# Cross-attention's output projection: a signal for each half unit, both additions ahead of both low parts, and the MLP norm's sum one unit later

## The reference

```python
u = rms_norm_2(h, norm_xattn_g[l])
mem_n = rms_norm_2(mem, norm_mem_g[l])
h = h + memory_cross_attention(u, mem_n, w_xq[l], w_xkv[l], w_xo[l])   # ends in o @ w_xo
u = rms_norm_2(h, norm_mlp_g[l])                                      # over the 1024 features
h = h + jnp.square(jax.nn.relu(u @ w_mlp1[l])) @ w_mlp2[l]
```

## Time and profile before

| | |
|---|---|
| Median of 3 runs | 2702.25 us |
| The profiled execution's own time | 2701.49 us |
| Its span in the profile | 2699.7 us |
| TensorE (PE) busy | 2619.4 us, 97%, 11814 matmuls |
| VectorE (DVE) busy | 1434.7 us, 53% |
| ScalarE (ACT) busy | 942.6 us, 35% |
| GpSimd (POOL) busy | 370.2 us, 14% |
| Mean granted TensorE clock | 0.986 of full speed |
| Share of PE in the chain that ended last | 88% |

### The profile page before, as it was taken

One profiled execution on the slowest core, in us unless ns is written; L12 is line 12 of the kernel. 1 busy time (PEld: TensorE's weight loads), 2 busy tenths in 40 slices (PEclk: granted clock), 3 DMA queues, 4 the chain that ended last, 5 costly groups with the idle time before them and its releaser, 6 DMA issues.

```text
span 2699.7 us, 32457 instructions
## 1 busy us (share of the span) xinstructions
PE 2619.4 (97%) x11814; PEld 2162.0 (80%) x11814; DVE 1434.7 (53%) x1719; ACT 942.6 (35%) x1364; POOL 370.2 (14%) x314
## 2 busy tenths in 40 slices
PE   7999999999999999999999999998788999899998
PEld 6888888888888888888888888886677788788887
DVE  7444356664443454434676444337865676552443
ACT  4222224432322232222443222233665434341332
POOL 2000111310001100001022000111463121200001
PEclk9999999999999999999999999999899999899999
DMA  4333332233333233333323333332322333133332
GB/s 139 100 100 89 100 82 80 80 100 95 99 95 94 85 109 100 93 98 83 87 70 100 99 98 91 99 87 67 85 62 52 118 97 98 50 106 101 94 98 81
DMA packets 487838, 247.22 MB, mean 92 GB/s; under 512 B 39873, under 2 KB 484550, under 8 KB 487494
## 3 DMA queue, kind: packets, MB, share of 16 engines
q1 hardware_dynamic: 487298, 245.75, 31.6%
q10 hardware_dynamic: 452, 0.32, 0.0%
HBM read 241.84 MB, written 4.19 MB: 91 GB/s over the span
## 4 chain that ended last, share of the span: by engine, by line
PE 88%; DVE 5%; POOL 3%; issue 2%; ACT 1%; DMA 0%; DVEq 0%; POOLq 0%; ACTq 0%
PE bank L653 14%; PE bank L655 14%; PE bank L654 14%; PE psT L653 9%; PE psT L655 9%; PE psT L654 9%; PE psS L653 3%; PE psS L654 3%; PE psS L655 3%; POOL zc L2320 2%; DVE wlo L1622 1%; POOL p L2331 0%; PE psT L722 0%; PE bank L1024 0%; PE bank L1023 0%
## 5 line engine op out<-in xcount | busy, mean ns | idle before, releaser
L1622 DVE TENSOR_TENSOR wlo<-raw,whi 128x1024 fp32r<-128x1024 f32 x466 | 623.4, 1339 | 465.0 <-ACT whi L1205 447.3
L653 PE MATMUL bank<-xhi,whi 128*128 128x512 f32 x1736 | 688.4, 397 | 26.9 <-DVE q2l L1939 9.0
L654 PE MATMUL bank<-xlo,whi 128*128 128x512 f32 x1736 | 680.3, 392 | 0.0
L655 PE MATMUL bank<-xhi,wlo 128*128 128x512 f32 x1736 | 680.2, 392 | 0.0
L1205 ACT ACTIVATE whi<-raw 128x1024 fp32r<-128x1024 f32 x463 | 484.2, 1049 | 321.8 <-PE psT L655 316.7
L653 PEld LDWEIGHTS bank<-xhi,whi 128*128 128x128 f32 x1736 | 328.8, 189 | 103.9 <-issue 11.3
L655 PEld LDWEIGHTS bank<-xhi,wlo 128*128 128x128 f32 x1736 | 328.6, 189 | 69.8
L654 PEld LDWEIGHTS bank<-xlo,whi 128*128 128x128 f32 x1736 | 329.3, 190 | 68.9 <-issue 2.0
L655 PE MATMUL psT<-hhi,wlo 128*128 128x512 f32 x704 | 273.9, 389 | 0.0
L653 PE MATMUL psT<-hhi,whi 128*128 128x512 f32 x704 | 273.9, 389 | 0.0
L654 PE MATMUL psT<-hlo,whi 128*128 128x512 f32 x704 | 273.9, 389 | 0.0
(11 more groups left out here) (466 smaller groups left out, 3451.5 us busy)
## 6 DMA issues: line engine op xcount, KB each, us to landing
raw<-in_ffn_wg SPq DMA_DIRECT2D x88, 512.0 KB
raw<-in_ffn_wu SPq DMA_DIRECT2D x88, 512.0 KB
raw<-in_ffn_wd SPq DMA_DIRECT2D x64, 512.0 KB
raw<-in_w_mlp SPq DMA_DIRECT2D x64, 512.0 KB
raw<-in_w_in SPq DMA_DIRECT2D x53, 512.0 KB
raw<-in_ffn_wd SPq DMA_DIRECT2D x32, 384.0 KB
raw<-in_w_in SPq DMA_DIRECT2D x24, 256.0 KB
raw<-in_w_out SPq DMA_DIRECT2D x11, 512.0 KB
```

The costliest lines, as they stand in the source:

```text
L653: pe.matmul(dest, a, rhs_hi(k), start=start and k == 0, stop=False)
L654: pe.matmul(dest, a, rhs_lo(k), start=False, stop=False)
L655: mm = pe.matmul(dest, b_, rhs_hi(k), start=False, stop=stop and k == tiles - 1)
L1622: dve.tensor_tensor(wlo[:, a:a + UNIT], raw[:, a:a + UNIT], whi[:, a:a + UNIT].bitcast(F32), ALU.subtract).then_inc(s_split, 1)
```

## The change

```diff
@@ tensor, output projection
                         mm = pe.matmul(xo_b[2 * (j % 2) + i], wl, chunk(a3h, k), start=False, stop=k == 3)
-                mm.then_inc(s_used, 1)
+                    mm.then_inc(s_used if i else d_pv, 1)
@@ tensor, four() of the MLP
                         unit(c + j, q, mlp_b[j], KC, *xk(), ready=ready)
-                        if first and ps == 0 and j == 0:
+                        if first and ps == 0 and j == 1:
                             pe.wait_ge(s_sq, (FINAL1 + 3) * KC)
                             pe.matmul(psO[:, :], ones[:, :], acc[:, :], start=True, stop=True).then_inc(s_ss, 1)
@@ vector, output projection
             for j in range(KC // 2):
-                split(C_XO + j + AHEAD, 0)
-                dve.wait_ge(s_used, C_XO + j + 1)
                 for i in range(2):
                     m = 2 * j + i
+                    if i:
+                        split(C_XO + j + AHEAD, 0)
+                        dve.wait_ge(s_used, C_XO + j + 1)
+                    else:
+                        dve.wait_ge(d_pv, TB + j + 1)
                     dve.tensor_tensor(chunk(x, m), xo_b[2 * (j % 2) + i], chunk(x, m), ALU.add).then_inc(s_x, 1)
-                    x_lo(FINAL1 + 2, m)
+                for i in range(2):
+                    x_lo(FINAL1 + 2, 2 * j + i)
```

More of the change, by code:

```diff
@@ L380, in build @@
         d_tl = sem("cross_probs_lo_ready")
-        d_pv = sem("cross_pv_done")
+        d_pv = sem("cross_pv_or_out_half_done")
         d_oh = sem("cross_out_hi_ready")
```

## The result

The changed kernel takes 2693.46 us, the median of 7 runs (2691.93 to 2695.60), against 2702.25 of before (7 runs, 2698.70 to 2702.58). The ratio is 0.9972 with a 95% interval of 0.9960 to 0.9984: faster, by 7.6 us (4.3 to 10.8). Measured again (experiment 9), the same kernel had 0.9975 (0.9966 to 0.9984). The profiled execution's span is 2691.6 us, 8.1 less than before.

What follows compares the result with a forecast made beforehand. TensorE bounds the kernel, never idle behind 2344 us, with 7.94 us winnable before u4. Starting u4 at 2353.6 instead of 2360.43 wins 6.8 us: 2702.25 - 6.8 = 2695.4 us, range 2693.5 to 2698.9.

Steps and rivals of the forecast that it cites:

- Chunk 7's low part behind u0's start: End of the projection on VectorE: ready at 2333.15 (2332.3 to 2333.9), ahead of tile 7 at 2334.63, closing u0's gaps.
- `var` to the end of u4's split: Inverse root behind the sum: takes 11.65 us, none of them TensorE's, so u4's split ends at 2353.46.
- both waits: VectorE's queue in the projection: 0.79 us behind each addition for ScalarE's high part, and blocking by GpSimd hidden in durations.
- The two parts of the queue: VectorE in the projection: early first-half signal and both additions ahead of both low parts close both gaps, 1.5 us margin.
- The sum: Moved behind u1, due at 2340.75: no wait (0 to 0.5 us); behind u0 it would have waited 3.6 us.
- its 2338.9: When GpSimd's 15 operations for the norm end, followed through with overlaps at the handovers; 2341.2 without any overlap.
- What was late next: Start of u4: waits 1.0 us for its split, about 0.1 more for first weights (0.8 to 1.6); u5 none.
- The clock did not fall: Rival: clock falls at u4's wait for some 6.6 us, losing 3.3 us of the gain; 2698.8 us, chance 6 in 100.
- VectorE was not late in part: Rival: blocking costs 0.3 us more per operation, chunk 7 2 us late, 1.9 us lost; 2697.4 us, 5 in 100.
- the pair of engines taking turns: Rival: VectorE and GpSimd, one at a time, need 7.39 us a unit; no change, 2703.2 us, 6 in 100.
- The slower case: Rival: clock falls at u4's wait and stays low 17.3 us, costing 8.6 us; 2704.1 us, 3 in 100.
- the case of no wait at u4: Rival: steps from `var` on are quicker, so u4 does not wait; 7.9 us won, 2694.3 us, 2 in 100.

Runs made afterwards that it cites:

- experiment 9: The changed kernel, unaltered, measured again on the same chip as three other runs: ratio 0.9975 to the kernel before.
- experiment 6: The kernel before, with GpSimd's squares and additions for the MLP norm replaced by one-column memsets giving the same signals: ratio 0.9970 to the kernel before.
- experiment 3: The changed kernel, but each low part directly behind its addition as before; signal, split's place and later sum kept: ratio 0.9983 to the kernel before.
- experiment 4: The changed kernel without the first half's signal: split first, wait for the whole unit, both additions, both low parts: ratio 0.9989 to the kernel before.
- experiment 5: The changed kernel with the split ahead of the first addition instead of between the two additions: ratio 0.9979 to the kernel before.
- experiment 7: The changed kernel with the norm's sum one more unit later, behind u2: ratio 1.0001 to the kernel before.
- experiment 8: The changed kernel with u4's split ahead of the inverse root, TensorE waiting for u0's eviction ahead of u4: ratio 0.9969 to the kernel before, both times.
- the half changes: The changed kernel without the low parts' order, without the first half's signal, or with the split ahead of the first addition: 0.9983, 0.9989, 0.9979 of before.

## Why the prediction was right

| Step | Forecast | Measured |
|---|---|---|
| First addition ahead of the second | 2.75 us | 2.75 us (2309.67, 2312.42) |
| Waits for `xlo` in u0 | none | none |
| Chunk 7's low part behind u0's start | 3.3 us (2.4 to 4.0) | 3.72 |
| `acc` complete behind u0's start | 9.0 us | 8.21 |
| `var` to the end of u4's split | 11.65 us | 11.66 (2340.48 to 2352.14) |
| u4's start behind u0's | 23.7 us | 23.66, 23.65 |
| Won | 6.8 us | 6.9 by the profile, 7.6 and 6.8 by the ratios |
| Clock behind u4's wait | 1.00 | 1.00 |

**VectorE is late because of GpSimd and ScalarE.** The prediction named both waits, and both are shown (experiment 6 and the lines beside it). The reading of GpSimd's, a low part of 1.48 us ending 0.55 behind the square and a split ending 1.07 behind `acc`, was the step the rest stood on. What the Trainium skill, "SBUF — State Buffer", section "Who interferes with whom", states and no row of before showed, that GpSimd's operation is the one blocked when VectorE's started first, is in the changed trace with a square of 1.84 us. For ScalarE the prediction left one wait of 0.79 us per unit; the changed kernel's waits list none for `xlo`.

**The two parts of the queue.** Right, and both needed (experiments 3 and 4); followed through in the same way the distances forecast were within 0.3 us for each. I had not given the split's place a price; it has one, 1.4 us (experiment 5).

**The sum.** The prediction said that behind u0 it would have waited 3.6 us; it waited 2.62, since GpSimd is done 0.8 us sooner than I had it (the rest is how the end of the last matmul is counted). The prediction gives no working for its 2338.9, so which term was too dear stays open. A likely one, as an estimate: a blocked square ends 0.90 us behind its blocker (2333.54 + 1.84 against 2332.17 + 2.31), and not the full 1.04, and all eight are blocked, which makes up to 8 x 0.14 = 1.1 us. It changed nothing, since the sum had 1.8 us to spare by my count and 2.7 in fact.

**What was late next.** u4's split, with 0.83 us of idle time and some 0.2 more for the restart. Experiments 7 and 8 show it from both sides.

**The rivals.** The clock did not fall, VectorE was not late in part, and the pair of engines taking turns did not hold VectorE to 7.4 us a unit. The slower case was a mechanism that exists: experiment 7 has the low spell. It was 7 us long there, from 2353 to 2360, came with a wait of 6.26 us, and cost 1.4 us behind u4's start, not the 8.6 of the forecast's case. Read from the earlier trace rows, the two low spells of before are 6.8 and 17.1 us long, where the prediction has 6.6 and 17.3; this moves no price by more than 0.1 us.

**The total.** 2695.4 was forecast and 2693.46 measured, at the very lower end of the range (2693.5 to 2698.9). The rest of 1.9 us is not explained by the change: measured again, the same kernel won 6.8. The mechanism is the one forecast, but that the median came out as low as the range goes, where the case of no wait at u4 stood, is luck of the runs: the wait was there.

## What to carry to other kernels

Read an operation's duration against its own minimum before calling it work: a low part of 1.48 us where 0.75 is usual is a wait that no view of waits lists. Where two engines block each other, the blocking need not go: here VectorE stayed blocked for 7.0 us, and the gain came from taking its waits for a third engine out of the queue without adding to the blocking, as the half changes did. The backlog is then with the engine off the path; count what that delays (here the sum). A sum that feeds a long chain should stand as late as its input forces and no later: one unit late costs nothing only until its chain is due, and then all of it.

## What the runs showed of the hardware

- VectorE with two SBUF inputs and GpSimd's operations exclude each other in both directions: a square of GpSimd takes 1.04 us alone, 1.30 to 1.48 against a low part, 1.84 against a split, and a blocked one ends 0.90 us behind its blocker; an addition that reads PSUM takes 0.68 to 0.69 us beside GpSimd's operations.
- TensorE's clock stayed at 2.4 GHz through single waits of 0.83, 1.51 and 2.62 us and fell to 1.2 GHz at the end of one of 3.52 and within one of 6.26 (0.64 in 2352 to 2354).
- Executions of equal work differ by 4.4 us at the same instruction 2300 us into the kernel (2326.61 to 2330.99 in twelve profiles), so a change of 1 us is seen in the profile's distances and not in the time.
